# Three layers on one core: a chunked recurrence in blocks of 32, and projections in another order

## The chip, the cores and the metric

One core of a Trainium2 chip runs the whole program. Everything is fp32. The metric is the time of one execution in device microseconds; the kernel before took 1384.18 us (median of 3 runs, 1381.27 to 1385.24).

## The reference, cut to what matters

Three layers over 512 tokens of width 1024. The first two are "x + gate * rmsnorm(mixer(modulated rmsnorm(x)))"; layer 1 (L = 0 in the code) has latent attention (MLA, 8 heads, queries and keys through small latents cq and ckv) and windowed attention (SWA: sq, sk, sv, 8 query heads, 2 key heads); layer 2 (L = 1) has differential and forgetting attention. The third (L = 2, the "Mixer") has three kinds of sparse attention, stick-breaking attention, and HGRN2, the gated recurrence that most of the change is about:

```
b    = cumsum(log_f) within a chunk                        # per head and key channel
att[t, s] = sum_d q[t, d] key[s, d] exp(b[t, d] - b[s, d]) for s <= t
o    = att @ v + (q * exp(b)) @ state
state = exp(b_last) * state + (key * exp(b_last - b))^T @ v
o    = o * rsqrt(mean(o^2) + eps) * norm_w * silu(z)       # 6 heads of 64
x    = layer_norm(ALPHA * x + mixed @ w_out) * ln_g + ln_b
```

## The kernel before, in words

Tokens are tiled in T = 4 tiles of 128 (P). Each engine has one program in its own order; they meet at semaphores. On VectorE, ScalarE and Pool every operation waits for the one before it (`link`, `give`, `own`), so their times add up. Weights come through a ring of three slots of 2 MB (`ring`), filled by SyncE in the order of `chunks`; a slot is filled again when the last job of the chunk that it held is done (`chunk_end`). Products of weights and activations are jobs in one fixed order (`pr_plan`), the same on all engines: TensorE fills a PSUM bank, VectorE or ScalarE empties it. Before and between attentions jobs go round eight banks, beside an attention and in the last stage round two.

Layer 1 (TensorE's part, lines 1036 to 1089): cq and ckv (token-major, contraction of 8 blocks); their normalised tiles transposed (`cqT`, `ckvT`, copied by ScalarE); uq with the transposes `mqT`; ukv with `mkT`; then `roped` sq with `sqT` and skv with `skT` (VectorE rotates a tile, TensorE transposes it one tile later, ScalarE copies); gate0's first tile; then the attention. In `attention` (lines 922 and 1374 and 2028) each step handles one head's scores of one tile: TensorE makes the scores of a later step (`LOOK` = 2 ahead), filler work (projections of other parts, by `SPREAD`), the transposes of the weights, filler again, and the output of the step before. Score s has to wait until score s - 2 is masked. So the first step of an attention issues three scores, or four where they go in pairs.

The Mixer's attention has 88 steps, 72 to 87 of them stick-breaking; their fillers end with the part of the output projection whose inputs are ready (`mE`, `ye`: 5 of 8 contraction blocks). `HG_EARLY` names the steps behind which ScalarE makes the exponentials of chunks 0 and 1 of the recurrence. `close_behind` is where VectorE finishes a group of heads and frees its output bank.

The Mixer's stage (TensorE lines 1143 to 1215, VectorE 2301 to 2357, ScalarE 1590 to 1608, Pool 1651 to 1706) handles HGRN2 in 4 chunks of 128 tokens and 3 pairs of heads. exp(b[t] - b[s]) is not split over a whole chunk, but by levels: on level l the tokens go in blocks of 2^(l+1), the second half of a block looks at the first, and both are scaled relative to the border. Pool makes the differences, ScalarE their exponentials, Pool the products with key and query: 7 operands Y (levels 0 to 6), in two sets used in turn. TensorE multiplies for each level the operand by itself in two blocks of HB = 64 for both heads of the pair (`level_products`: 28 products of 64x64, and 2 for level 6, between the blocks); VectorE masks 7 of them (`levels`, 0 or 1) and adds them up into `att`, seven operations a pair, one of them the copy of level 6. TensorE then makes the chunk's outputs (`outputs`), and between these steps, `feed`, the rest of the output projection of the tile before (3 transposes and 6 products). VectorE then normalises the chunk's output (the "tail": copy, square, sum, rsqrt, scale, norm weights, gate), updates the state, and handles the layer norm of the tile two before (`output_tile`: ScalarE sums and squares, VectorE waits and scales, Pool applies ln_g and ln_b).

Of the kernel before, what the change touches and what calls it, by code (L numbers as in the profile page):

```python
# [31 lines left out]
P = 128  # L32
# [24 lines left out]
HB = 64  # L57
HP = 3
GW = NLEV * HB
# [16 lines left out]
def constants():  # L76
# [16 lines left out]
    for l in range(NLEV - 1):  # L93
        h = 1 << l
        lev.append((s // (2 * h) == t // (2 * h)) & (s % (2 * h) < h) & (t % (2 * h) >= h))
# [94 lines left out]
def pr_plan():  # L190
# [10 lines left out]
    def transposes(name):  # L201
        jobs.extend((name, i) for i in range(T))

# [131 lines left out]
HG_EARLY = (78, 84)  # L335
# [6 lines left out]
def two_block_kernel(nc, A, C, out):  # L342
# [15 lines left out]
    with ExitStack() as ctx:  # L358
# [67 lines left out]
        def carve(sizes):  # L426
            at, got = 0, {}
            for name, shape, rows in sizes:
# [35 lines left out]
        Y = [arena[:, o:o + NLEV * 384].rearrange("p (l m t) -> p l m t", l=NLEV, m=3)  # L464
             for o in (0, 2688)]
        slot = ring_slots(chunks)
        spare = ring[:, slot["w", "hi"], :]
        qb = [v.rearrange("p (m t) -> p m t", m=3) for v in (arena[:, 5376:5760], spare[:, 2048:2432])]
        kb = [v.rearrange("p (m t) -> p m t", m=3) for v in (arena[:, 5760:6144], spare[:, 2432:2816])]
# [4 lines left out]
        dec = [arena[:, 6528 + 4 * r:6531 + 4 * r] for r in range(2)]  # L474
# [11 lines left out]
        ktok = stage[:, 1536:3072].rearrange("p (b n) -> p b n", b=2)  # L486
        rtok = stage[:, 0:1024].rearrange("p (b n) -> p b n", b=2)
# [70 lines left out]
        gs_s = sem("gs_s")  # L558
        ho_done = sem("ho_done")
        hof = sem("hof")  # L560
        st_s = sem("st_s")
        ln_s = sem("ln_s")
        ln_q = sem("ln_q")
# [25 lines left out]
        def steps(L):  # L589
# [191 lines left out]
        def _(pe):  # L781
# [263 lines left out]
            for r in range(2):  # L1045
                b = begin(("relrow", r))
                pe.matmul(b[0:NSH, 0:320], tbl, onehot_r[:, 320 * r:320 * r + 320],
                          start=True, stop=True).then_inc(pr_done, 1)
            for i in range(T):
                if i == 0:  # L1050
                    drained(pe, ("ckv", T - 1))
                transposes(("cqT", i), [cqn[:, i, k * P:k * P + P] for k in range(3)])
            for i in range(T):
                transposes(("ckvT", i), [ckvn[:, i, k * P:k * P + P] for k in range(2)])
            drained(pe, ("ckvT", T - 1))
            for w, src, K, n, tr_name, tile in (("uq", a0["cqT"], 3, 384, "mqT", qtok),
                                                ("ukv", a0["ckvT"], 2, 512, "mkT", ktok)):
                W = weights(("w", w))
                for i in range(T + 1):
                    if i < T:  # L1060
                        for g in range(2):
                            token_major((w, i, g), W, i, n * g, n, src, K)
                    if i >= 1:
# [5 lines left out]
            def roped(name, n, nt, tile):  # L1069

                W = weights(("w", name[0]))
                for i in range(T + 1):
# [5 lines left out]
                    if i < T:  # L1078
                        token_major((name[0], i), W, i, 0, n)
                    if i >= 1:  # L1080
# [3 lines left out]
            roped(("sq", "sqT"), 512, 4, rtok)  # L1084
            roped(("skv", "skT"), 256, 1, rktok)
            whole_tile(("gate0", 0, 0))
            banks_back(pe, ("gate0", 0, 0))
# [55 lines left out]
            for c in range(T):  # L1143
                t = slice(c * P, c * P + P)
                pe.wait_ge(yr_s, c + 1)
                if c < T - 1:
                    transposes(("kbT", c), [kb[c % 2][:, m, :] for m in range(3)])

                def level_products(m):
                    n = c * HP + m  # L1150
                    if n >= 2:
                        pe.wait_ge(gm_s, n - 1)
                    for l in range(NLEV):
                        for j in range(2):
                            u = slice(HB * j, HB * j + HB)
                            for r in range(2):
                                q = slice(MN * r, MN * r + MN)
                                if l < NLEV - 1:
                                    a = b_ = Y[c % 2][q, l, m, u]
                                else:  # L1160
                                    w = slice(c * P + HB * j, c * P + HB * j + HB)
                                    a, b_ = a2["key"][q, m, w], a2["hq"][q, m, w]
                                pe.matmul(GB[n % 2][u, r, HB * l:HB * l + HB], a, b_, start=True, stop=True)
                    for r in range(2):
                        q = slice(MN * r, MN * r + MN)
                        mm = pe.matmul(GB[n % 2][0:HB, r, GW:GW + HB], Y[c % 2][q, NLEV - 1, m, 0:HB],
                                       Y[c % 2][q, NLEV - 1, m, HB:P], start=True, stop=True)
                    mm.then_inc(g_done, 1)

                def outputs(m):  # L1170
# [6 lines left out]
                    if c > 0:  # L1177

                        pe.matmul(OB[c % 2][:, m * P:m * P + P], qb[c % 2][:, m, :], state[:, m, :],
                                  start=True, stop=False)  # L1180
                    pe.wait_ge(gs_s, n + 1)
                    for r in range(2):
# [36 lines left out]
        def _(act):  # L1219
# [215 lines left out]
            def exponentials(c):  # L1435
# [3 lines left out]
                link(act.activation(Y[c % 2], Y[c % 2], ACT.Exp))  # L1439
                link(act.activation(kb[c % 2], kb[c % 2], ACT.Exp))  # L1440
                link(act.activation(qb[c % 2], a2["b"][:, :, t], ACT.Exp))
                if c >= 2:
                    act.wait_ge(pr_free[bank_of[prn["st", c - 2]]], nth[prn["st", c - 2]])
                give(act.activation(dec[c % 2], a2["b"][:, :, c * P + P - 1:c * P + P], ACT.Exp), ye_s, c + 1)

            def output_tile(i):
                drained(act, ("y", 2, i, 1))
                yb = ybuf2[:, i % 2, :]
                say(act.activation(tok[:, i, :], yb, ACT.Copy, accum_out=ss[:, 0:1]), sq_s, "sq_s")
                hear(mean_s, "mean_s")  # L1450
                say(act.activation(tok[:, i, :], yb, ACT.Square, bias=lam[:, 7:8], accum_out=ss[:, 0:1]), sq_s, "sq_s")
                rsqrt()
# [54 lines left out]
            for i in range(T):  # L1507
                for g in range(2):
# [12 lines left out]
            for i in range(T):  # L1521
                b = take(act, ("sqT", i))
                release(copy(a0["sqT"][:, :, i * P:i * P + P], heads(b[:, :])), ("sqT", i))
# [66 lines left out]
            for c in range(T + 1):  # L1590
# [9 lines left out]
                else:  # L1600
# [6 lines left out]
                if c < T:  # L1607
                    rsqrt(HGH)
# [15 lines left out]
        def _(pool):  # L1624
# [26 lines left out]
            def differences(c):  # L1651

                bc = a2["b"][:, :, c * P:c * P + P]
                if c >= 2:
                    pool.wait_ge(g_done, HP * (c - 1))
                    pool.wait_ge(ho_done, HP * (c - 1))
                for l in range(NLEV):
                    h = 1 << l
                    yl = Y[c % 2][:, l, :, :]
# [4 lines left out]
                tt(kb[c % 2], widen(last, P), bc, ALU.subtract).then_inc(y_s, 1)  # L1664
                pool.wait_ge(y_s, c + 1)

            def operands(c):
# [3 lines left out]
                for l in range(NLEV):  # L1671
                    h = 1 << l
                    yl = Y[c % 2][:, l, :, :]
                    own(tt(halves(yl, l, 0), halves(yl, l, 0), halves(a2["key"][:, :, t], l, 0), ALU.mult))
                    own(tt(halves(yl, l, h), halves(yl, l, h), halves(a2["hq"][:, :, t], l, h), ALU.mult))
                own(tt(kb[c % 2], kb[c % 2], a2["key"][:, :, t], ALU.mult))
                tt(qb[c % 2], qb[c % 2], a2["hq"][:, :, t], ALU.mult).then_inc(yr_s, 1)
# [22 lines left out]
            for c in range(T + 1):  # L1700
                if c + 2 < T:
# [728 lines left out]
```

## Time and profile before

| | |
|---|---|
| median of 3 runs | 1384.18 us |
| the profiled execution: its time, its span | 1384.93 us, 1383.4 us |
| busy: TensorE, VectorE, ScalarE, Pool | 1218.8, 557.7, 430.6, 106.0 us |
[...]

Durations are from that one execution. TensorE is busy in 88% of the span, but not evenly: the page's slices show nines through the layers and 6 to 8 in the last three of 40, where VectorE and Pool are busiest. An f32 matmul shows as two instructions. [...]

### The profile page before, as it was taken

What the parts mean: (1) busy time and instruction counts of PE and PEld (TensorE: products, weight loads), DVE (VectorE), ACT (ScalarE), POOL (GpSimd) and SP (SyncE); (2) the same over time, 40 slices, a digit from 0 to 9 for tenths busy, and PEclk for the clock granted to TensorE, in tenths of its full rate; (3) what the DMA queues carried; (4) which work ended last, traced back from release to release, by engine and by line L of the source; (5) the groups of instructions that cost most, each with busy time, mean ns of one, the idle gap of its engine ahead of it and who ended that gap; (6) DMA issues with size and microseconds to landing.
All of it is one profiled execution on the core that took longest, in us unless ns stands there. A gap on an engine that the chain in (4) does not pass through costs nothing.

```text
span 1383.4 us, 15153 instructions
## 1 busy us (share of the span) xinstructions
PE 1218.8 (88%) x5264; PEld 679.4 (49%) x5264; DVE 557.7 (40%) x1428; ACT 430.6 (31%) x1096; POOL 106.0 (8%) x138
## 2 busy tenths in 40 slices
PE   4879989999889898979999989989998999878654
PEld 1555454555554443334455555555453656545442
DVE  3234323334554311335442431122236532663885
ACT  0133014444451102232243322214343544660122
POOL 0000000000001000000000000000000000461752
PEclk8889989999998999999999989989999899998776
DMA  9321234562003412432111005241111011000001
GB/s 348 104 92 31 94 129 174 184 225 48 0 1 99 69 17 61 89 102 59 52 61 61 1 12 136 62 167 46 46 35 35 23 62 62 1 1 31 1 17 46
DMA packets 60402, 99.71 MB, mean 72 GB/s; under 512 B 12084, under 2 KB 22145, under 8 KB 60328
## 3 DMA queue, kind: packets, MB, share of 16 engines
q1 hardware_dynamic: 54514, 93.58, 22.1%
q10 hardware_dynamic: 5814, 5.18, 1.2%
q8 instruction: 43, 0.70, 0.2%
q14 instruction: 31, 0.25, 0.1%
HBM read 96.60 MB, written 4.08 MB: 73 GB/s over the span
## 4 chain that ended last, share of the span: by engine, by line
PE 74%; DVE 14%; ACT 5%; issue 2%; DMA 2%; ACTq 1%; DVEq 0%; SPq 0%
PE PR L905 32%; PE PT L798 6%; PE OB L935 6%; PE SC L957 6%; PE PR L798 5%; PE OB L798 4%; PE SC L798 4%; PE PT L972 3%; PE PR L860 3%; DVE stage L1735 2%; DMA ring<-in_w_ada 2%; DVE d L1735 1%; DVE tok L1735 1%; DVE ring L1735 1%; PE PR L813 1%
## 5 line engine op out<-in xcount | busy, mean ns | idle before, releaser
L905 PE MATMUL PR<-ring,hT 128*128 128x512 f32 (+1 forms) x784 | 376.4, 594 | 4.4 <-ACT hT L1244 3.5
L905 PEld LDWEIGHTS PR<-ring,hT 128*128 128x128 f32 x784 | 137.2, 198 | 104.8 <-issue 87.5
L1410 ACT ACTIVATE stage<-stage,nmax 128x256 f32<-128x256 f32 (+7 forms) x200 | 103.7, 519 | 268.1 <-DVE nmax L2087 237.8
L935 PEld LDWEIGHTS OB<-arena,pts 128*128 128x128 f32 (+3 forms) x880 | 129.1, 196 | 97.0 <-issue 76.2
L905 PE MATMUL PR<-hT,ring 128*128 128x512 f32 (+1 forms) x304 | 151.0, 622 | 0.0
L1643 POOL TENSOR_TENSOR arena<-arena 128x192 f32<-128x192 f32 (+1 forms) x118 | 78.6, 666 | 827.4 <-PE OB L935 758.0
L935 PE MATMUL OB<-arena,pts 128*128 128x64 f32 (+4 forms) x880 | 127.2, 273 | 9.2 <-ACT pts L1244 9.1
L957 PE MATMUL SC<-arena 64*128 64x256 f32 (+15 forms) x432 | 111.1, 447 | 10.2 <-DVE nmax L2087 10.2
L1244 ACT ACTIVATE pts<-PT 128x256 f32<-128x256 f32 (+7 forms) x200 | 80.7, 404 | 86.0 <-PE PT L972 63.5
L972 PEld LDWEIGHTS PT<-ident,stage 128*128 128x128 f32 (+3 forms) x440 | 58.6, 144 | 96.7 <-issue 69.5
L972 PE MATMUL PT<-ident,stage 128*128 128x128 f32 (+3 forms) x440 | 85.3, 285 | 13.1 <-DVE stage L1743 9.1
L2087 DVE CUSTOM_DVE_ANT_0 stage<-SC,causal 128x128 f32<-128x128 f32 (+3 forms) x96 | 47.1, 491 | 104.6 <-issue 55.0
L905 PEld LDWEIGHTS PR<-hT,ring 128*128 128x128 f32 (+1 forms) x304 | 51.4, 190 | 53.0 <-issue 51.7
L2087 DVE CUSTOM_DVE_ANT_0 stage<-SC,arena 128x128 f32<-128x128 f32 (+7 forms) x72 | 27.9, 388 | 96.1 <-PE SC L957 94.4
L957 PEld LDWEIGHTS SC<-arena 64*128 64x128 f32 (+2 forms) x432 | 45.9, 189 | 21.1 <-DVE nmax L2087 10.7
L798 PE MATMUL PR<-ring,hT 128*128 128x512 f32 (+5 forms) x160 | 50.6, 472 | 3.9 <-ACT hT L1287 2.0
L1739 DVE TENSOR_SCALAR t<-PR 128x512 f32<-128x512 f32 (+3 forms) x29 | 17.4, 600 | 85.3 <-PE PR L905 74.3
L798 PE MATMUL PT<-ring,hT 128*128 128x512 f32 (+4 forms) x144 | 50.0, 502 | 0.0
L860 PE MATMUL PR<-ring,tok 128*128 128x512 f32 x80 | 44.6, 690 | 6.0 <-ACT tok L1244 5.9
L798 PE MATMUL SC<-ring,hT 128*128 128x512 f32 (+3 forms) x144 | 48.0, 491 | 0.0
L1264 ACT ACTIVATE t<-t 128x512 f32<-128x512 f32 (+3 forms) x32 | 16.8, 525 | 73.7 <-DVE t L1739 73.6
L798 PEld LDWEIGHTS PR<-ring,hT 128*128 128x128 f32 x160 | 28.0, 199 | 23.3 <-issue 16.5
(346 smaller groups left out, 1332.1 us busy)
## 6 DMA issues: line engine op xcount, KB each, us to landing
ring<-in_w_ada SPq DMA_DIRECT2D x12, 2048.0 KB, 8.3
ring<-in_od_w_in SPq DMA_DIRECT2D x8, 2048.0 KB, 17.1
ring<-in_w_in SPq DMA_DIRECT2D x5, 1536.0 KB, 7.0
ring<-in_ev_w_in SPq DMA_DIRECT2D x3, 2048.0 KB, 7.8
ring<-in_w_in SPq DMA_DIRECT2D x3, 2048.0 KB, 9.9
ring<-in_ev_w_out SPq DMA_DIRECT2D x2, 2048.0 KB, 10.1
ring<-in_od_w_out SPq DMA_DIRECT2D x2, 2048.0 KB, 7.9
ring<-in_w_out SPq DMA_DIRECT2D x2, 2048.0 KB, 7.9
```

The lines of the kernel that those rows point to most:

```text
L798: mm = pe.matmul(dst, lhs(k), rhs(k), start=(k == 0), stop=(k == K - 1))
L860: mm = pe.matmul(b[:, :], tok[:, i, k * P:k * P + P], W[:, k, :], start=(k == 0), stop=(k == EARLY - 1))
L905: mm = pe.matmul(dst, l, r, start=(k == 0), stop=(k == KT - 1))
L935: mm = pe.matmul(ob[:, h * w:h * w + w], pts[0:rows_, v % 2, n * P:n * P + P], vb, start=(n == 0), stop=(n == len(blocks) - 1))
L957: pe.matmul(SC[s % 2][:, 0:n], q, k, start=True, stop=True).then_inc(s_done, 1)
L972: tr = pe.transpose(PT[v % 2][0:w, b * P:b * P + P], pb[:, s % NP, b * P:b * P + w], ident[:, :])
L1244: return act.activation(dst, src, ACT.Copy, scale=scale)
L1410: give(act.activation(pb[:, s % NP, 0:n], zm[:, s % 2, 0:n], ACT.Exp, bias=nmax[:, row, c:c + 1], scale=-1.0, accum_out=rsum[:, row, c:c + ...
L1643: return pool.tensor_tensor(dst, a, b, op)
L1735: return dve.tensor_tensor(dst, a, b, op)
L1739: return dve.tensor_scalar(dst, a, s1, None, op0)
L2087: give(dve.tensor_tensor_reduce(out=z, in0=SC[s % 2][:, 0:n], in1=mask, scale=-scale, scalar=start, op0=ALU.add, op1=ALU.min, accum_out=nm ...
```

## The change

Three edits. First, layer 1's projections: sq's weights come third, and its four tiles and their transposes go between the transposes of cq and ckv and the uq tiles, in a buffer of their own (`sqtok`, in tok); gate0's first tile goes ahead of the last skT. Second, in the attentions of layer 1 and the Mixer the first step looks one score ahead; the exponentials of chunks 0 and 1 come behind steps 75 and 82; a stick-breaking group is closed ahead of the step's scores; the norm's weights are multiplied onto the gate when that is made. Third, the Mixer's stage: blocks of 32, six levels masked (0 to 4 and the diagonal), and levels 5 and 6 copied into `att` by ScalarE; three sets of operands, so that Pool works through chunks 2 and 3 without waiting for the chunk just before; ScalarE squares the chunk's output from PSUM; the layer norm in steps between the head pairs, scaled by ScalarE; Pool's output tiles all behind chunk 3.

```diff
-HB = 64
-GW = NLEV * HB
+HB = 32
+GW = 6 * HB
-    transposes("cqT")
-    transposes("ckvT")
+    chunk(("w", "sq"), [("sq", 0)] + [("cqT", i) for i in range(T)] + [("sq", 1)] + [("ckvT", i) for i in range(T)]
+          + [("sqT", 0), ("sq", 2), ("sqT", 1), ("sq", 3), ("sqT", 2)])
...
+            if (w, i) == ("uq", 0):
+                u.append(("sqT", T - 1))
...
-    chunk(("w", "sq"), with_transposes("sq", "sqT"))
-    chunk(("w", "skv"), with_transposes("skv", "skT"))
+    chunk(("w", "skv"), with_transposes("skv", "skT")[:-1])
     jobs.append(("gate0", 0, 0))
+    jobs.append(("skT", T - 1))
...
-HG_EARLY = (78, 84)
+HG_EARLY = (75, 82)
...
-                upto = min(need + LOOK, s_all[-1])
+                upto = min(need + (1 if v == mine[0] and L != 1 else LOOK), s_all[-1])
...  (TensorE, layer 1)
-            banks_back(pe, ("gate0", 0, 0))
+            banks_back(pe, ("skT", T - 1))
...  (TensorE, level_products)
+                    for l in range(GW // HB):
+                        for b in range(P // HB):
+                            u = slice(HB * b, HB * b + HB)
+                            for r, q in enumerate(halves):
+                                ...
+                                pe.matmul(G[u, r, HB * l:HB * l + HB], k_, q_, start=True, stop=True)
+                    for j in range(2):
+                        for r, q in enumerate(halves):
+                            u = slice(64 * j, 64 * j + HB)
+                            pe.matmul(G[u, r, GW:GW + HB], y[5][q, m, u], y[5][q, m, 64 * j + HB:64 * j + 64],
+                                      start=True, stop=True)
+                    for r, q in enumerate(halves):
+                        mm = pe.matmul(G[0:64, r, GW + HB:GW + HB + 64], y[6][q, m, 0:64], y[6][q, m, 64:P],
+                                       start=True, stop=True)
...  (TensorE, outputs)
                     pe.wait_ge(gs_s, n + 1)
+                    pe.wait_ge(gc_s, n + 1)
...  (ScalarE)
+            def cross_blocks(c, m):
+                ...
+                act.wait_ge(gm_s, n + 1)
+                for j in range(2):
+                    u = slice(64 * j, 64 * j + HB)
+                    link(copy(w[u, :, 64 * j + HB:64 * j + 64], G[u, :, GW:GW + HB]))
+                give(copy(w[0:64, :, 64:P], G[0:64, :, GW + HB:GW + HB + 64]), gc_s, n + 1)
...
+            exponentials(2)
+            act.wait_ge(att_zero, 1)
+            for c in range(T):
                 ...      (kbT's and mT's copies as before)
+                cross_blocks(c, 0)
+                if c >= 2:
+                    norm_sum(c - 2)
+                cross_blocks(c, 1)
+                if c == 0:
                     for g in range(2):
                         mixed_ahead(T - 1, g)
-                if 1 <= c < T - 1:
-                    exponentials(c + 1)
                 if c >= 2:
-                    output_tile(c - 2)
+                    norm_square(c - 2)
+                if c == 2:
+                    exponentials(3)
+                cross_blocks(c, 2)
+                if c >= 2:
+                    norm_factor()
+                act.wait_ge(ho_done, HP * (c + 1))
+                give(act.activation(d2[:, 0:384], OB[c % 2][:, 0:384], ACT.Square), ho_sq, c + 1)
+                rsqrt(HGH)
+                if c >= 2:
+                    norm_scale(c - 2)
...  (Pool)
-                if c >= 2:
-                    pool.wait_ge(g_done, HP * (c - 1))
-                    pool.wait_ge(ho_done, HP * (c - 1))
+                if c >= 3:
+                    pool.wait_ge(g_done, HP * (c - 2))
+                    pool.wait_ge(ho_done, HP * (c - 2))
...  (VectorE)
+            def level_sums(n):
+                ...
+                give(tt(gm, G[:, :, 0:GW], ... levels ..., ALU.mult), gm_s, n + 1)
+                link(tt(gm[:, :, 0:3 * HB], gm[:, :, 0:3 * HB], gm[:, :, 3 * HB:6 * HB], ALU.add))
+                link(tt(gm[:, :, 0:HB], gm[:, :, 0:HB], gm[:, :, HB:2 * HB], ALU.add))
+                for b in range(P // HB):
+                    u = slice(HB * b, HB * b + HB)
+                    ins = tt(w[u, :, u], gm[u, :, 0:HB], gm[u, :, 2 * HB:3 * HB], ALU.add)
...  (chunk c)
+                level_sums(c * HP)
+                if c >= 2:
+                    norm_mean()
+                level_sums(c * HP + 1)
+                if c >= 2:
+                    norm_variance()
+                level_sums(c * HP + 2)
+                if c >= 2:
+                    norm_factor()
```

## Rows read from the trace of the kernel before

**Rows 1.** the page's chain of waits, shares of the span by engine

```profile
PE 74%; DVE 14%; ACT 5%; issue 2%; DMA 2%; ACTq 1%; DVEq 0%; SPq 0%
```

**Rows 2.** table by stretch: PE, PEld, DVE, ACT, POOL busy us, clock, DMA

```profile
1300.00:1383.00 83.00, 45.11 (x468) 28.41 (x466) 62.30 (x127) 18.39 (x40) 40.08 (x45) 0.73 0.07 26
```

**Rows 3.** TensorE's timeline, layer 1's projections: start, us, work [idle before]

```profile
89.33 0.66 PE L813 MATMUL SC<-ident,stage 128*128 128x128 f32 x3 [2.50 <-DVE arena L1735]
...
98.26 4.18 PE L798 MATMUL SC<-ring,arena 128*128 128x384 f32 x6 [4.87 <-ACT arena L1502]
102.23 4.56 PE L798 MATMUL PT<-ring,arena 128*128 128x384 f32 x12
...
139.33 7.03 PE L798 MATMUL SC<-ring,hT 128*128 128x512 f32 x16
...
171.05 5.30 PE L798 MATMUL SC<-ring,hT 128*128 128x256 f32 x16
176.19 3.62 PE L798 MATMUL PT<-ring,hT 128*128 128x256 f32 x16
...
199.82 0.80 PE L957 MATMUL SC<-arena 96*128 96x128 f32 x2 [3.58 <-DVE nmax L2087]
```

**Rows 4.** waits from 88 to 215 us: total us, times, longest

```profile
PE SC L813 <- DVE stage L1735: 3.8, 2, 2.3
```

**Rows 5.** the page's DMA issues: count, KB each, us to landing

```profile
ring<-in_ev_w_in SPq DMA_DIRECT2D x3, 2048.0 KB, 7.8
```

**Rows 6.** TensorE's and ScalarE's timelines, end of the Mixer's attention

```profile
1243.44 1.11 PE L813 MATMUL PR<-ident,tok 128*128 128x128 f32 x4 [4.82 <-DVE tok L1735]
...
1233.71 2.44 ACT L1439 ACTIVATE arena<-arena 128x2688 f32<-128x2688 f32 x1
```

**Rows 7.** VectorE's timeline: a row beside Pool, a head pair

```profile
1321.77 2.40 DVE L1735 TENSOR_TENSOR stage<-stage 128x384 f32<-128x384 f32 x3
...
1342.25 1.09 DVE L1735 TENSOR_TENSOR stage<-PT,grow 128x896 f32<-128x896 f32 x1
1343.38 0.28 DVE L2310 COPY ring<-PT 64x128 f32<-64x128 f32 x1
1343.69 1.21 DVE L1735 TENSOR_TENSOR stage<-stage 128x384 f32<-128x384 f32 x3
1344.94 0.61 DVE L1735 TENSOR_TENSOR ring<-stage 64x128 f32<-64x128 f32 x2
```

**Rows 8.** TensorE's timeline of the Mixer's stage

```profile
1258.43 1.04 PE L1163 MATMUL SC<-arena 64*64 64x64 f32 x56
...
1301.19 0.66 PE L1184 MATMUL OB<-arena,ring 128*128 128x64 f32 x4 [0.35 <-DVE ring L1735]
...
1346.64 1.77 PE L1163 MATMUL PT<-arena 64*64 64x64 f32 x56
...
1348.55 3.78 PE L996 MATMUL PR<-ring,hT 128*128 128x512 f32 x4
...
1352.95 1.94 PE L996 MATMUL PR<-ring,hT 128*128 128x512 f32 x4
```

**Rows 9.** VectorE's and TensorE's timelines, where the chunks and their tails begin

```profile
1280.09 0.56 DVE L2328 COPY d<-OB 128x384 f32<-128x384 f32 x1
...
1288.32 1.09 DVE L1735 TENSOR_TENSOR stage<-PT,grow 128x896 f32<-128x896 f32 x1
...
1312.90 1.09 DVE L1735 TENSOR_TENSOR stage<-SC,grow 128x896 f32<-128x896 f32 x1 [1.14 <-PE SC L1166]
...
1357.15 0.56 DVE L2328 COPY d<-OB 128x384 f32<-128x384 f32 x1
...
1364.87 0.87 PE L987 MATMUL PR<-ident,tok 128*128 128x128 f32 x3 [7.60 <-DVE tok L1735]
```

**Rows 10.** ScalarE's timeline, one operation of the last norm

```profile
1352.48 1.15 ACT L1451 ACTIVATE tok<-ring,lam 128x1024 f32<-128x1024 f32 x1 [9.44 <-DVE lam L1739]
```

**Rows 11.** Pool's timeline, the multiplications of chunk 3

```profile
1320.21 10.19 POOL L1643 TENSOR_TENSOR arena<-arena 128x192 f32<-128x192 f32 x14 [4.03 <-ACT arena L1444]
```

More of the change, by code:

```diff
@@ L92, in constants @@
     s, t = np.arange(P)[:, None] % HB, np.arange(HB)[None, :]
-    for l in range(NLEV - 1):
+    for l in range(GW // HB - 1):
         h = 1 << l
@@ L473, in two_block_kernel @@
         kbT = arena[:, 6144:6528]
-        dec = [arena[:, 6528 + 4 * r:6531 + 4 * r] for r in range(2)]
+        dec = [arena[:, 6528 + 4 * r:6531 + 4 * r] for r in range(3)]
         state = arena[:, 6656:7040].rearrange("p (m e) -> p m e", m=3)
@@ L558, in two_block_kernel @@
         gs_s = sem("gs_s")
+        gc_s = sem("gc_s")
         ho_done = sem("ho_done")
@@ L1048, in _, with swa_transposes @@
                           start=True, stop=True).then_inc(pr_done, 1)
+            W = weights(("w", "sq"))
+            def swa_transposes(i):
+                drained(pe, ("sq", i))
+                transposes(("sqT", i), [sqtok[:, i % 2, k * P:k * P + P] for k in range(4)])
+            token_major(("sq", 0), W, 0, 0, 512)
             for i in range(T):
@@ L1052, in _ @@
                 transposes(("cqT", i), [cqn[:, i, k * P:k * P + P] for k in range(3)])
+            token_major(("sq", 1), W, 1, 0, 512)
             for i in range(T):
                 transposes(("ckvT", i), [ckvn[:, i, k * P:k * P + P] for k in range(2)])
+            for i in range(T - 1):
+                swa_transposes(i)
+                if i + 2 < T:
+                    token_major(("sq", i + 2), W, i + 2, 0, 512)
             drained(pe, ("ckvT", T - 1))
@@ L1079, in roped @@
                         token_major((name[0], i), W, i, 0, n)
+                    if i == T and name[0] == "skv":
+                        whole_tile(("gate0", 0, 0))
                     if i >= 1:
@@ L1507, in _ @@
             for i in range(T):
+                b = take(act, ("sqT", i))
+                release(copy(a0["sqT"][:, :, i * P:i * P + P], heads(b[:, :])), ("sqT", i))
+            for i in range(T):
                 for g in range(2):
@@ L1699, in _ @@
             operands(1)
-            for c in range(T + 1):
-                if c + 2 < T:
-                    differences(c + 2)
-                if c + 2 < T:
-                    operands(c + 2)
-                if 1 <= c < T:
-                    output_tile(c - 1)
+            for c in range(2, T):
+                differences(c)
+                operands(c)
+            for i in range(T - 1):
+                output_tile(i)
         @block.vector
@@ L2094, in attention @@
                     finish_gates()
-                    if r_:
+                    if r_ and not stick_end:
                         close_behind(v - 1)
@@ L2177, in _ @@
                 if i >= 2:
+                    used(dve, ("sqT", i - 2))
+                b = take(dve, ("sq", i))[:, :].rearrange("p (n w) -> p n w", n=NH)
+                u, w = rope(None, b, NH, MN, cosh_[:, i, :], sinh_[:, i, :])
+                dst = sqtok[:, i % 2, :].rearrange("p (j v d) -> p v j d", j=4, v=2)
+                four = lambda z: z.rearrange("p (v j) d -> p v j d", v=2)
+                for kv in range(2):
+                    ins = tt(dst[:, kv, :, :], four(u)[:, kv, :, :], four(w)[:, kv, :, :], ALU.add)
+                    if kv == 0:
+                        link(ins)
+                release(ins, ("sq", i))
+            for i in range(T):
+                if i >= 2:
                     used(dve, ("mqT", i - 2, 1))
```

197 lines of the change are left out of this document (95 added, 102 removed).

## The prediction, made before the changed kernel ran

> **What bounds the kernel now.** I read the chain of waits first, by engine: TensorE holds 74% of it and VectorE 14% [rows 1]. The reader should take from it that there are two kinds of stretch. [...] Then TensorE's timeline for the projections of layer 1 (L = 0 in the code), and VectorE's and TensorE's for the Mixer's stage.
>
> **Part 1: projections of layer 1.** TensorE waits 2.50 us for the normalised ckv before the first transposes, and 4.9 us before uq's first product. That product runs slow: its 6 instructions take 4.18 us, where the next 12 take 4.56: 1.9 lost [rows 3]. The last transposes of sq and of skv wait 3.8 us in two waits [rows 4], and after the first of them skv's first product takes 5.30 against 3.62: 1.7 lost [rows 3]. Sum: 2.5 + 4.9 + 1.9 + 3.8 + 1.7 = 14.8 us. In the new order an sq product of 6.9 us (the 128x512 pattern of rows 3) stands in front of the cq transposes, another in front of the ckv transposes, so ScalarE's copies of cqT and ckvT (8 us) run beside sq(1) and sq(2); the last sqT stands behind uq(0), and gate0's first tile in front of the last skT. Each gap has at least 3.9 us of products in it, against chains on VectorE of at most 2.6 us (an sq tile's rotation, the longest). Added: a wait for the last skT's copy on ScalarE before the first scores, 0.6 us, behind which all of TensorE stands. Net 14.2.
>
> Transfers: sq's 2 MB now load third, into the slot that the modulation's fourth chunk leaves, some 45 us before use. SyncE's queue is past skv's wait at about 120. The gate's first 2 MB are issued behind the last ukv product, about 17 us before use, behind two rows of 0.5 MB; 7.8 us to landing is what such a chunk takes [rows 5]. Hidden; if not, a few us.
>
> First step with two scores: TensorE now waits 3.58 us at the third score, because VectorE first finishes the gate [rows 3]. Without it the filler's first part runs in that time and the first transpose comes when its weights are ready, some 4.7 us behind the gate's tile instead of 6.8; the score (0.4) still has to be done. Gain 1.7; in the Mixer's attention the same with smaller tiles, 0.4.
>
> **Part 2: the end of the Mixer's attention.** TensorE stands 4.82 us for VectorE's closing of a stick-breaking group. In front of it ScalarE made chunk 1's exponentials: 2.44 us and three small ones, 3.9 in all [rows 6]. Now these come two steps earlier, where VectorE and ScalarE both idle behind slow products, and the group is closed ahead of the next tail. That takes 4.8 away. Chunk 0's exponentials come three steps earlier, in steps of 2.7 us that have no slack on ScalarE: a new stall of up to 3.9, I take 3.0. The four products with the norm's weights (0.56 us each on VectorE) move here beside TensorE's work: 0, at most 2.3. Net gain 1.8 (bounds: loss 3, gain 5).
>
> **Part 3: the Mixer's stage.** Per head pair VectorE took 1.09 + 0.28 + 1.21 + 0.61 with gaps = 3.33 us [rows 7]. From the 896 column and the 128 column rows an operation costs about 0.15 + 0.00105 us a column. The new seven (384, 192, 64, and four of 64 columns) then cost 0.55 + 0.35 + 5 x 0.22 + gaps 0.2 = 2.2. So 12 x 1.1 = 13 us leave VectorE. But they are not on the path all the time: in chunk 1 TensorE's last outputs waited only 0.35 us for VectorE [rows 8], so its own row of work (outputs, level products, six projection products at half clock and then full clock) was as long: from 1288.32 + 3.35 to 1301.85, 10.2 us. That is what is late next.
>
> Price of the new level products. Before: 56 instructions of 64x64 take 1.04 us at the high level, 1.77 at the low one: 18.6 and 31.6 ns each [rows 8]. As a + b and a + 2b that is 5.6 fixed and 13.0 that goes with the clock. Now there are 108 instead of 60, nearly all of 32 columns. If nothing of the 13.0 shrinks: 2.0 us fast, 3.4 slow. If it shrinks with both sizes (to a quarter): 1.0 and 1.3. I take half, 12 and 19 ns: 1.3 and 2.0, where it was 1.1 and 1.9: nothing. No row has such a tile; the ends go into the range.
> [...]
>
> Tail of a chunk (outputs read until the gated result): 384 column operations are 0.56 us each [rows 9]. A copy, a square and the weights' product leave VectorE, ScalarE's square (0.5) comes: net 1.1. Pool's work no longer falls on all of it; with Pool beside it three sums took 2.40 instead of 1.21 [rows 7]. The state's 6 small operations become 4 wider ones, 0.3.
>
> Chunk by chunk, on starts of operations of VectorE (the last: TensorE) [rows 7 to 9]:
> - Chunk 0 (until 1280.09) is TensorE's: ten projection products. The first now wait for the copies of mixed behind the second head pair on ScalarE instead of for VectorE: 1.5 earlier (bounds 0 and 5, the latter if the clock no longer falls).
> - 1280.09 to 1288.32, 8.2: now 4.9. Gain 3.3.
> - Chunk 1 until its outputs are there, 1301.85 [rows 8], 13.5: now 2.2 + 0.7 beside Pool + 10.2 = 13.1. Gain 0.4.
> - to 1312.90, 11.05: now tail 4.4, residual half 0.7, then kbT's transposes and a level product, 2.9. Gain 3.0.
> - Chunk 2 and its tail, to 1342.25, 29.35. ScalarE's order is mT's copy, cross blocks, the norm's sum (1.15 [rows 10]), cross blocks, its square, the exponentials of chunk 3 (3.9), cross blocks. VectorE waits for the mean until about T+5.1 and for the square until T+8.1; the exponentials end at T+12.0, the third cross blocks at 12.9, the outputs at 13.5, the factor's part on VectorE at 15.0. Pool multiplies only from T+12.0 and needs 12.4 (14 in 10.19 us [rows 11] and two more). TensorE waits for that at T+24.4, and the first products of chunk 3 take 1.9: T+26.4. Gain 2.95. So a new wait, for Pool, takes most of what VectorE saves.
> - Chunk 3 to 1357.15, 14.9: now 3.8 + 9.8 + 0.6. Gain 0.7.
> - Tail 3 to 1364.87, 7.7: now 4.7. Gain 3.0.
> - The rest, 18.5 us, goes by TensorE's 12 products and the last norm, which are unchanged: 0.
> Sum of part 3: 14.85.
>
> All: 14.2 + 2.1 + 1.8 + 14.9 = 33.0 us. The profiled execution took 1384.93, 0.75 over the median of 1384.18: 1384.93 - 33.0 = 1351.9, or 1351 on the median.
>
> **Rivals.**
> Small products cost as much as large ones. TensorE's path holds about nine groups of level products in the stage, the two of chunk 0 at the high level (+0.7), seven at the low one (+1.4), of which some 2 are hidden: +9, 1360. For: the fixed cost per instruction is real and the count doubles. Against: the part that goes with the clock, 13 of 18.6 ns, is array time, and half as many columns stream and load.
> The clock stays up. VectorE's shorter pauses could spare TensorE the half clock: 3.78 us for four instructions of a projection against 1.94 [rows 8], in chunks 0 to 3 and the end, and the low prices of the level products: 10 us less, 1341. Against: it still idles over 4 us in each tail.
> The first part is not had in full, because the gate's or the modulation's chunk lands late or banks come back late: 7 to 9 us less, 1359.
> The other side: the 32 column tiles don't run beside each other. It lies in level products alone. At the 0.43 us that one full instruction takes (6.9 us for 16 [rows 3]), a quarter of it for 128 columns in place of 512, 0.11 us, a head pair takes 11.7 us and 12 of them 125 more: about 1476. It decides from 33 / 12 = 2.8 us more for a head pair, 36 ns an instruction. Against: the 64x64 products already come every 18.6 ns, on four tiles.
>
> **How the numbers follow.** Forecast 0.56; small products dear 0.19; clock 0.12; part 1 short 0.09; the other side 0.04. All but the last are faster by over 0.3% (4.2 us, which is about what a measurement of this kernel can tell); 0.01 is for sums of mishaps that end within it: 0.95, 0.01, 0.04. The range goes from the clock's case to the dear products with some of part 1 missing: 1340 to 1365.
>
> **What would show it.** Part 1: no TensorE gap over 1.5 us between 86 us and the first scores, these at about 181 instead of 195.6. Part 2: the 4.8 us wait gone, one of some 3 near step 75. Part 3: VectorE near 2.2 us a head pair, VectorE starts of chunks 1 and 2 some 24 us apart become some 21; TensorE or Pool, not VectorE, ends the waits in chunks 2 and 3; an idle time of TensorE for Pool before chunk 3. I am wrong if a head pair's level products exceed 2.5 us at the low level, or if chunk 3 starts less than 24 us or more than 29 after chunk 2.

## The result, and the profile after

The changed kernel takes 1368.01 us (median of 4, 1365.65 to 1372.01) against 1384.71 us before: ratio 0.9877, 95% interval [0.9848, 0.9905]. The same kernel timed again beside later experiments gave 1363.70 (6 runs, 1360.40 to 1368.97) against 1385.11: 0.9855 [0.9832, 0.9878]. So it gains 17 to 20 us where 33 were forecast. The forecast of 1351 was wrong, and so was its range of 1340 to 1365.

The profiled execution has a span of 1363.9 us, 19.5 less than before's 1383.4. Its chain of waits by engine, against [rows 1]:

```profile
PE 77%; DVE 11%; ACT 5%; issue 2%; DMA 2%; ACTq 1%; POOL 1%; DVEq 0%; SPq 0%; POOLq 0%
```

The last 83 us in the table by stretch, against [rows 2]:

```profile
1280.90:1363.90 83.00, 50.39 (x880) 31.60 (x880) 48.76 (x130) 29.55 (x72) 27.73 (x26) 0.75 0.07 27
```

VectorE fell from 62.3 to 48.8 us and ScalarE rose from 18.4 to 29.6: the work was moved as the diff says. Before, this was a stretch in which VectorE was busy longer than TensorE; now TensorE is, 50.4 against 48.8. In the last three of the page's 40 slices TensorE's busy tenths went from 6, 5 and 4 to 8, 6 and 5, its granted clock from 7, 7 and 6 to 8, 7 and 7. TensorE's timeline of layer 1's projections, against [rows 3]:

```profile
86.74 7.13 PE L804 MATMUL SC<-ring,hT 128*128 128x512 f32 x16
...
137.73 0.61 PE L819 MATMUL PR<-ident,stage 128*96 128x128 f32 x4 [1.21 <-ACT arena L1270]
...
172.69 7.10 PE L911 MATMUL PR<-ring,hT 128*128 128x512 f32 x16 [1.63 <-DVE stage L1800]
...
180.33 0.71 PE L963 MATMUL SC<-arena 96*128 96x128 f32 x4 [0.43 <-ACT arena L1270]
...
184.41 0.33 PE L978 MATMUL PT<-ident,stage 128*128 128x128 f32 x1 [2.37 <-ACT stage L1436]
```

The gaps of 2.50 and 4.87 us are gone; the first scores come at 180.33 instead of 195.63, 15.3 earlier. The end of the Mixer's attention, on TensorE, against [rows 6]:

```profile
1182.81 0.69 PE L978 MATMUL PT<-ident,stage 128*128 128x128 f32 x2 [3.20 <-ACT stage L1408]
1183.30 2.77 PE L911 MATMUL PR<-ring,hT 128*128 128x384 f32 x4
...
1193.22 2.04 PE L866 MATMUL PR<-ring,tok 128*128 128x512 f32 x2 [0.83 <-ACT tok L1270]
...
1236.41 0.46 PE L819 MATMUL PR<-ident,tok 128*128 128x128 f32 x1 [3.61 <-DVE x L1808]
...
1252.31 0.99 PE L1184 MATMUL SC<-arena 64*32 64x32 f32 x94
```

The first level products start at 1252.31 against 1258.43, only 6.1 earlier. At step 75 of the Mixer's attention, just ahead of the first of these rows, the lead over before had been 12.6. So in the stretch of part 2, which was to gain 1.8, 6.5 were lost.

The Mixer's stage, against [rows 7 to 9]: VectorE's starts of chunks 1, 2 and 3, one head pair, and TensorE in front of and behind chunk 3.

```profile
1279.36 0.56 DVE L1800 TENSOR_TENSOR stage<-PT,grow 128x384 f32<-128x384 f32 x1
...
1280.83 2.64 DVE L1800 TENSOR_TENSOR ring<-stage 32x64 f32<-32x64 f32 x4
...
1299.01 0.56 DVE L1800 TENSOR_TENSOR stage<-SC,grow 128x384 f32<-128x384 f32 x1 [0.76 <-PE SC L1191]
...
1304.28 0.56 DVE L1800 TENSOR_TENSOR stage<-PT,grow 128x384 f32<-128x384 f32 x1
1304.87 0.62 DVE L1800 TENSOR_TENSOR stage<-stage 128x192 f32<-128x192 f32 x2
1305.52 0.97 DVE L1800 TENSOR_TENSOR ring<-stage 32x64 f32<-32x64 f32 x4
...
1325.00 0.56 DVE L1800 TENSOR_TENSOR stage<-PT,grow 128x384 f32<-128x384 f32 x1 [4.11 <-PE PT L1191]
1325.59 2.65 DVE L1800 TENSOR_TENSOR stage<-stage 128x192 f32<-128x192 f32 x2
```

The last of these rows in a narrower view, and what Pool does at that time:

```profile
1325.98 2.26 DVE L1800 TENSOR_TENSOR stage<-stage 128x64 f32<-128x64 f32 x1
...
1325.59 2.57 POOL L1710 TENSOR_TENSOR x<-ring,arena 128x1024 f32<-128x1024 f32 x1
```

```profile
1323.14 1.16 PE L1184 MATMUL PT<-arena 64*32 64x32 f32 x92 [8.05 <-POOL arena L1710]
...
1324.82 1.16 PE L1184 MATMUL SC<-arena 64*32 64x32 f32 x92
...
1345.01 0.52 PE L993 MATMUL PR<-ident,tok 128*128 128x128 f32 x3 [4.53 <-DVE tok L1800]
```

| stretch | before | after | gain | forecast |
|---|---|---|---|---|
| first level products to chunk 1 | 29.9 | 27.1 | 2.8 | 4.8 |
| chunk 1 to 2 | 24.6 | 19.7 | 4.9 | 3.4 |
| chunk 2 to 3 | 29.4 | 26.0 | 3.4 | 2.95 |
| chunk 3 to TensorE behind its tail | 22.6 | 20.0 | 2.6 | 3.7 |
| rest | 18.5 | 18.9 | -0.4 | 0 |

Sum 13.3 against 14.85. A head pair takes VectorE 2.2 us as forecast (0.56, 0.62 and 0.97 from 1304.28; beside Pool the last is 2.64 and the middle one 2.65). The 108 instructions of a head pair's level products (54 in the kernel, each two in the trace) take 1324.82 - 1323.14 = 1.68 us at the low level (granted clock 0.50 from 1323.1 to 1326), from the first of one pair to the first of the next: 15.6 ns each. And the new wait for Pool is there, 8.05 us.

### The profile page after: what moved, and what is told of

Its sections match the earlier page's. It is cut to its first block, busy times and chain, and to the rows that moved or that the text cites. A ratio compares the mean times of both kernels' runs of the same rounds, so it can differ in the third digit from the quotient of the medians.

```text
span 1363.9 us, 16366 instructions
## 1 busy us (share of the span) xinstructions
PE 1218.7 (89%) x5840; PEld 677.9 (50%) x5840; DVE 538.3 (39%) x1412; ACT 445.1 (33%) x1140; POOL 105.5 (8%) x138
## 4 chain that ended last, share of the span: by engine, by line
PE 77%; DVE 11%; ACT 5%; issue 2%; DMA 2%; ACTq 1%; POOL 1%; DVEq 0%; SPq 0%; POOLq 0%
PE PR L911 33%; PE OB L941 6%; PE SC L963 6%; PE PT L804 5%; PE PR L804 5%; PE OB L804 5%; PE SC L804 4%; PE PT L978 3%; PE PR L866 3%; DMA ring<-in_w_ada 2%; PE PR L1002 1%; DVE tok L1800 1%; DVE stage L1800 1%; POOL arena L1710 1%; DVE arena L2025 1%
## 5 line engine op out<-in xcount | busy, mean ns | idle before, releaser
L911 PEld LDWEIGHTS PR<-ring,hT 128*128 128x128 f32 x784 | 138.0, 199 | 106.6 <-issue 89.4
L1710 POOL TENSOR_TENSOR arena<-arena 128x192 f32<-128x192 f32 (+1 forms) x90 | 60.5, 673 | 823.8 <-PE OB L941 761.4
L804 PE MATMUL PR<-ring,hT 128*128 128x512 f32 (+5 forms) x176 | 55.9, 473 | 3.9 <-ACT hT L1313 2.0
L963 PEld LDWEIGHTS SC<-arena 64*128 64x128 f32 (+2 forms) x432 | 46.3, 192 | 15.6 <-issue 4.4
L804 PEld LDWEIGHTS PR<-ring,hT 128*128 128x128 f32 x176 | 30.4, 195 | 25.5 <-issue 18.8
L804 PE MATMUL PT<-ring,hT 128*128 128x512 f32 (+4 forms) x128 | 42.9, 491 | 0.0
```

The source lines that it names most:

```text
L804: mm = pe.matmul(dst, lhs(k), rhs(k), start=(k == 0), stop=(k == K - 1))
L911: mm = pe.matmul(dst, l, r, start=(k == 0), stop=(k == KT - 1))
L963: pe.matmul(SC[s % 2][:, 0:n], q, k, start=True, stop=True).then_inc(s_done, 1)
L1710: return pool.tensor_tensor(dst, a, b, op)
```

## The experiments

Each run gives two readings: the median against the kernel before on the same chip (one kernel's runs spread over 4 to 14 us), and the trace. Kernels that share their code up to some instruction are aligned on its k-th occurrence; "lead" is the difference of the two times there. Where a stretch of one trace is compared with the same stretch of another, what the two had gained or lost ahead of it drops out.

**The three parts alone.** The kernel before with one part of the diff each.

> The kernel before with part 1 alone: the projections of layer 1 in the new order, everything else as before. The changed kernel's trace has its first scores 15.3 us earlier than before (180.3 against 195.6), but its lead is smaller 200 to 700 us later, with the same waits, because the granted clock stays low longer after them. Theory A (clock by chance of place): first scores 15 us earlier again, and of these 11 to 15 are left at the end: 1370 to 1374 against 1384.7. Rival B (a cost that the new order causes further on, in a transfer or a bank that comes later): the same five stretches lose the same 5 us, at the same instructions as in the changed kernel: 1374.5. My forecast before the result, 14.2, gives 1370.5.

> The kernel before with part 2 alone: chunk 0's exponentials at step 75 and chunk 1's at 82 in place of 78 and 84, and the end of a stick-breaking group put ahead of the next scores. Theory A (part 2 costs): a wait of some 3 us of TensorE near step 75 with half the clock behind it, and the 4.82 us wait gone: first level products 4 to 7 us later than before, 1389 to 1391. Forecast of the prediction: 1.8 faster, 1383. Rival B: the loss of 6.5 us in the changed kernel came from the rest of it (VectorE's tails beside Pool, the four products with the norm's weights), then this kernel is within 2 us of the kernel before.

> The kernel before with part 3 alone: the Mixer's stage rebuilt, with its three sets of operands and the four products with the norm's weights in the attention, chunk 0's and 1's exponentials still at steps 78 and 84. Theory A: the stage is 13.4 us shorter as in the changed kernel's trace, and the attention's end is as before: 1371 to 1373. Rival B (the norm's weights and the wider Pool work cost part of the 6.5 us at the end of the attention): first level products 2 to 4 us later than before, 1374 to 1376. The prediction's 14.85 gives 1370.

| kernel | median | before | ratio [95%] | effect |
|---|---|---|---|---|
| part 1 | 1370.07 | 1384.44 | 0.9899 [0.9877, 0.9921] | -14.0 |
| part 2 | 1389.77 | 1384.44 | 1.0044 [1.0029, 1.0059] | +6.1 |
| part 3 | 1372.77 | 1384.44 | 0.9921 [0.9898, 0.9944] | -10.9 |

The effects (one minus the ratio, of 1384.44) add up to 18.8 us, as much as the whole change. Part 1's first scores came at 180.09, 15.5 earlier. Part 3's span was 15.6 less, of which a lead of 2.8 was there at step 75, before its stage began; the other 12.8 lie inside the interval of its median. Part 2 is the surprise. Its timeline of TensorE:

```profile
1190.17 0.69 PE L972 MATMUL PT<-ident,stage 128*128 128x128 f32 x2 [3.20 <-ACT stage L1382]
...
1200.58 2.04 PE L860 MATMUL PR<-ring,tok 128*128 128x512 f32 x2 [0.83 <-ACT tok L1244]
...
1222.67 1.56 PE L860 MATMUL PR<-ring,tok 128*128 128x512 f32 x2 [2.44 <-ACT tok L1244]
...
1243.67 0.48 PE L813 MATMUL PR<-ident,tok 128*128 128x128 f32 x1 [3.61 <-DVE x L1743]
```

The same waits as in the changed kernel (3.20, 0.83, 3.61), without any of part 3. From step 75 to the level products its lead over before goes from +5.3 to -1.1, 6.4 lost, against 6.5 in the changed kernel. So the loss is part 2's own, and theory A holds. (The +5.3 before step 75 stands on identical code; see the clock below.)

**Which step is dear.**

```
-HG_EARLY = (75, 82)
+HG_EARLY = (78, 82)
```

> The changed kernel with chunk 0's exponentials at step 78, where the kernel before had them, and chunk 1's still at 82. Theory A (the step 75 is dear: a wait of 3.2 us and then 14 us at half the clock): the stall near step 75 is gone, the 4.82 us wait stays away, first level products 5 to 8 us earlier than in the changed kernel: 1360 to 1363 against its 1368. Rival B (the stall only moves to step 78, as TensorE has no slack there either): within 1.5 us of the changed kernel, 1367 to 1369.

1371.79 us, 0.9902 [0.9879, 0.9925]: no better. The trace says why: the stall at 75 went (lead over the changed kernel from +2.4 to +10.8), and behind step 82 all of it was lost (+0.7). ScalarE and Pool there:

```profile
1213.91 2.44 ACT L1466 ACTIVATE arena<-arena 128x2688 f32<-128x2688 f32 x1 [8.01 <-POOL ring L1710]
...
1188.32 24.60 POOL L1710 TENSOR_TENSOR arena<-arena 128x192 f32<-128x192 f32 x30 [14.67 <-ACT arena L1471]
1212.99 0.83 POOL L1710 TENSOR_TENSOR ring<-arena 128x384 f32<-128x384 f32 x1
```

Pool works 25.5 us on `operands(0)` and `differences(1)`, the products of chunk 0 and the differences of chunk 1, between the two exponentials. With four steps between them ScalarE stands 8.01 us at its head of queue, and TensorE 6.84 behind it. So the two steps are tied: a second exponential at 82 needs the first well ahead of 78, and my theory A for this run left that out.

```
-HG_EARLY = (75, 82)
+HG_EARLY = (78, 84)
```

> The changed kernel with both exponentials back at steps 78 and 84; the end of a stick-breaking group still ahead of the next scores. The run with step 78 and 82 showed ScalarE 8.01 us waiting for Pool, which needs 25.5 us between the two. Theory A (where ScalarE's and Pool's work falls is the whole cost of part 2, the early close is good): from step 75 to the first level products 6 to 9 us less than the changed kernel, 1360 to 1362 against 1368. Rival B (the early close itself costs: TensorE's wait of 3.61 us for VectorE's closed tile was made by it): 2 to 4 us less only, 1364 to 1366.

The second of this pair keeps (78, 84) and also puts the closing of a group back:

```
-                    if stick_end:
-                        close_behind(v - 1)
...
-                    if r_ and not stick_end:
+                    if r_:
```

> The changed kernel without part 2: steps 78 and 84, and the stick-breaking group closed where it was. Theory A: from step 75 to the first level products as in the run of part 3 alone (a wait of 5.2 us for VectorE near 1238, but no wait of 3.2 near step 75): 5 to 6.5 us less than the changed kernel, 1362 to 1363. Rival B (the early close itself costs): this one is faster than the kernel with 78 and 84 and the early close by 2 to 4 us, 1360 to 1362.

With the early close 1357.40 us, 0.9822 [0.9798, 0.9846]; without it 1361.61, 0.9839 [0.9814, 0.9863]. The stall of 3.20 us is gone in both traces. TensorE's waits near the second exponentials, with the early close and then without it:

```profile
1225.40 0.66 PE L978 MATMUL PT<-ident,stage 128*128 128x128 f32 x4 [1.49 <-ACT stage L1408]
1228.90 0.48 PE L819 MATMUL PR<-ident,tok 128*128 128x128 f32 x1 [2.85 <-DVE x L1808]
```

```profile
1233.84 1.12 PE L819 MATMUL PR<-ident,tok 128*128 128x128 f32 x4 [5.16 <-DVE tok L1800]
```

The early close turns one wait of 5.16 us into two of 1.49 and 2.85. The stretches of the traces:

| kernel | step 75 to the level products | step 75 to the end of the span |
|---|---|---|
| before | 80.6 | 205.6 |
| part 2 alone | 87.0 | 212.4 |
| changed | 87.1 | 198.7 |
| 78 and 84, early close | 80.5 | 191.7 |
| 78 and 84, closed where it was | 81.1 | 191.8 |

So the steps cost 6.6 us up to the level products. Behind the stall 8.4 had been lost; 1.8 come back, because the later waits are shorter in the changed kernel. The early close gains 0.6 there and 0.1 by the end: nothing that can be told apart. Part 2's loss is the steps'. By the ratios the first of the pair is 0.0033 to 0.0055 below the changed kernel, 4.6 to 7.6 us, which agrees with the traces' 6.6 to 6.9. Between the two of the pair the intervals overlap.

**The wait for Pool.** ScalarE makes chunk 3's exponentials in its idle time at the end of chunk 1.

```
+                if c == 1:
+                    exponentials(3)
...
-                if c == 2:
-                    exponentials(3)
```

> The changed kernel with one move: ScalarE makes chunk 3's exponentials behind the last cross blocks of chunk 1, where it idles 4.17 us, and not in chunk 2. Pool can then multiply some 15 us earlier. Theory A (Pool ends the wait before chunk 3, as the prediction said; what is late next is TensorE's own work, VectorE idles 4.11 us there): chunk 3 starts 22 to 23 us behind chunk 2 where it took 26.0, so 3 to 4 us less, 1364 to 1365. Rival B (contention): Pool's 16 operations now fall beside VectorE's tail of chunk 1, whose small operations take up to 2.7 times as long, and give back 2 to 3 us: within 1.5 us of 1368.

1358.64 us, 0.9822 [0.9791, 0.9852]. TensorE in front of chunk 3:

```profile
1308.45 0.99 PE L1184 MATMUL PT<-arena 64*32 64x32 f32 x94
...
1309.73 0.99 PE L1184 MATMUL SC<-arena 64*32 64x32 f32 x94
```

No wait for Pool, and the granted clock is 1.00 from 1308.4 to 1311: 108 instructions in 1.28 us, 11.9 ns each. The lead over the changed kernel is 6.4 us all through chunks 0 and 1 (from the clock of the layers before) and 10.8 at TensorE's last projection products: 4.4 are the move's. By the end of the span it is 5.5 (193.2 us from step 75 against 198.7). The other 1.0 lies behind TensorE's last product, where the traces here took 9.2 to 10.9 us, so it may not be the move's. Beside Pool the tail of chunk 1 gives back 0.8 up to the first level products of chunk 2; the lead is down to 4.3 some 8 us later and back at 6.2 before chunk 3. So the loss that rival B named is there for a while, but it does not last.

**Two scores in the first step.**

```
-                upto = min(need + (1 if v == mine[0] and L != 1 else LOOK), s_all[-1])
+                upto = min(need + LOOK, s_all[-1])
```

> The changed kernel with three scores again in the first step of each attention. Prediction: 1.7 us later behind the first step of layer 1 and 0.4 in the Mixer's. The changed kernel's trace gave 2.3 in the first and nothing in the second, where TensorE waits 2.90 us all the same. Theory A: 2.3 later in layer 1, within 0.3 in the Mixer's apart from the clock: 1370. Rival B (two scores save nothing, the 2.3 was the clock): both within 0.5.

1367.88 us, 0.9884 [0.9854, 0.9914], the same within its interval. Its first step of layer 1, from the first scores to the first value product, is 0.55 us longer in the trace (10.76 against 10.21). Against before it is 2.3 shorter in the changed kernel, but 1.8 of that are there with three scores too: the wait for the third score is 2.78 us behind the new order of part 1, where it was 3.58, and the rest was clock. In the Mixer's attention nothing can be told apart. Neither theory had the size.

**Both moves together, and the changed kernel again.**

> The changed kernel unchanged, timed again beside the two others. Theory A (the 5 us that its first profiled run lost between the first value product and step 75 are granted clock that differs from run to run): median 1365 to 1369, the distance between the same two instructions other than 974.7 us by up to 5, with TensorE's idle time in the stretch of layer 1 still 28 us. Rival B (they are a fixed cost of the new order): 974 to 976 again.

> The changed kernel with both moves that helped: exponentials of chunks 0 and 1 at steps 78 and 84, and those of chunk 3 behind the last cross blocks of chunk 1. Theory A (they lie in different stretches and add up: 8.0 of the one, 4.4 of the other by the traces): 1354 to 1357. Rival B (chunk 3's come beside a chunk 1 that is later relative to Pool's differences, so ScalarE waits for Pool and the gain of the second is lost): 1359 to 1361.

> As the kernel with both moves, and three scores again in the first step of the Mixer's attention, two in layer 1's alone. Theory A (two scores cost 1.5 us there: the wait for VectorE is 2.9 us either way, and less work is left beside it): 1.5 us less than the kernel with both moves, 1352 to 1355. Rival B (that 1.5 was the clock of single runs): the same as that kernel within 1.

With both moves 1351.15 us (1345.88 to 1356.89) against 1385.11: 0.9756 [0.9733, 0.9779]. Beside it the changed kernel ran at 1363.70, so they bring 12.5 us. From step 75 to the end of the span its trace takes 186.3 us, 12.3 less than the changed kernel's; the two moves alone took 6.9 and 5.5 off, 12.4 together. That is the best version here. Three scores in the Mixer's first step gave 1357.09 (1345.85 to 1359.89), 0.9788 [0.9760, 0.9816]: no gain. Between two value products around that step it takes 117.6 us, with two scores 117.8: the 1.5 that I had read was the clock. A warning comes with these sums. The changed kernel took 198.66 and 198.65 us from step 75 to the end in its two traces, but this last kernel took 189.6, 3.3 more than the one with two scores, though they differ only in a step 250 us ahead. So one trace of the last stretch is good to some 3 us, and that 12.3 meets 12.4 is in part luck.

**The clock.** The stretch between the first value product of layer 1 and one of the next layer's, in the tables of four kernels (before, part 1 alone, the changed kernel, the changed kernel again):

```profile
208.20:567.00 358.80, 330.35 (x1280) 175.71 (x1279) 130.32 (x339) 117.87 (x313) 6.95 (x2) 0.96 0.29 84
```

```profile
190.80:554.40 363.60, 335.69 (x1279) 178.43 (x1278) 130.23 (x339) 117.87 (x313) 6.95 (x2) 0.95 0.29 83
```

```profile
190.60:552.30 361.70, 333.74 (x1279) 177.72 (x1278) 130.31 (x339) 117.94 (x313) 6.95 (x2) 0.96 0.29 82
```

```profile
191.50:551.70 360.20, 331.84 (x1279) 176.50 (x1278) 130.28 (x339) 117.86 (x313) 6.95 (x2) 0.96 0.29 82
```

TensorE's idle time is 28.5, 27.9, 28.0 and 28.4 us, and VectorE's and ScalarE's work is the same to 0.1. What grows is TensorE's busy time: the same instructions at a lower granted clock. One place shows it best. The same product behind the same wait, before and in part 2 alone, where the code up to there is identical:

```profile
795.69 1.57 PE L905 MATMUL PR<-ring,hT 128*128 128x512 f32 x2 [1.04 <-ACT hT L1244]
797.05 1.06 PE L972 MATMUL PT<-ident,stage 128*128 128x128 f32 x4
797.91 2.72 PE L905 MATMUL PR<-ring,hT 128*128 128x512 f32 x4
```

```profile
793.02 1.10 PE L905 MATMUL PR<-ring,hT 128*128 128x512 f32 x2 [1.04 <-ACT hT L1244]
793.95 0.60 PE L972 MATMUL PT<-ident,stage 128*128 128x128 f32 x4
794.39 1.88 PE L905 MATMUL PR<-ring,hT 128*128 128x512 f32 x4
```

In the one the granted clock is 0.50 for 2.5 us and more from 797, behind a wait of 1.04 us (0.68 in the 4 us from 797), in the other it is 1.00 in the same 4 us: 1.7 us between them. From the first value product to step 75 the seven traces of kernels with the changed kernel's code there took 968.8 (twice), 971.3, 971.4, 972.2, 974.7 and 975.0: the first profiled run of the changed kernel, 974.7, was nearly the slowest, and before's own 969.7 lies inside (the two kernels with its code there: 967.2 and 967.4). The second trace of the changed kernel is one of the two at 968.8. Between the two traces of the changed kernel TensorE's busy time there went from 911.9 to 904.6 us and its idle time from 62.8 to 64.2. So theory A holds: the 5 us lost there are no fixed cost. One thing stays open. In the stretch of layer 1 alone three traces of the old order took 358.5 to 358.8, ten of the new 360.1 to 364.9. Of these ten the eight with two scores in the first step took 360.1 to 360.2 (three) or 361.6 to 361.9 (five), some 1.6 apart, as much as one fall of the clock cost above; the two with three scores took 363.6 and 364.9, so the first step may have a part in it. The idle time is the same, so it is clock too, but why the new order should always meet it later I did not settle. What makes the clock fall in one run and not in another the traces do not show.

## Why the prediction was wrong

Right: what bounds each stretch (with the last 83 us as the one where VectorE was busy longer, 62.3 us of them against TensorE's 45.1 [rows 2]), the direction, part 1, VectorE's price of a head pair, the wait for Pool with its place (8.05 us in front of chunk 3). Wrong: the sum, by 13 to 16 us. The parts alone miss by 7.9 (part 2), 4.0 (part 3), 1.5 (two scores) and 0.2 (part 1).

- **Part 1**, 14.2 forecast: 14.0 [10.9, 17.0] alone, 15.5 at its first scores. Held, though the agreement to 0.2 is in part luck: the first scores gained more than forecast, and the clock took some of it in layer 1's stretch. Up to the first scores TensorE has no new wait for a transfer or a bank, so the rival of a first part not had in full falls. "No gap over 1.5 us" was missed slightly (1.63, and 2.37 behind the scores).
- **First step with two scores**, 1.7 and 0.4: 0.55 and nothing. The wait of 3.58 us that it was to save had become shorter by part 1 already, and 2.37 us of wait, now for ScalarE, were left.
- **Part 2**, 1.8 gained: 6.1 lost. This is the step that failed, more than half of the error, and outside my own bound of a loss of 3. "A new stall of up to 3.9, I take 3.0" had the stall (3.20) and left out what comes behind it: from there to 1199 the granted clock is 0.50, and the lead falls from 12.6 to 6.4 by 1193.22. I had charged such a stretch elsewhere (1.9 behind a gap of 4.87) but not here. "That takes 4.8 away" failed too: 3.61 of the 4.82 us of wait are left. Read from the trace, VectorE's last chain for the group is as long as before or longer: its operations (0.96, 1.90 and 1.30 us, the middle one a scan) took 0.79, 1.58 and 0.90 before. They run beside Pool, which ScalarE's earlier exponentials started earlier (`operands(1)` at 1219 to 1235). That Pool is the reason for the wait is argued and not shown: with the exponentials back at 78 and 84 the chain was as fast as before, and the waits were 1.49 and 2.85. And I asked only what the exponentials delay, not what they are tied to: Pool's 25.5 us between them.
- **Part 3**, 14.85: 13.3 in the trace, 10.9 [7.8, 14.1] alone. By stretch it was 2.0 short up to chunk 1, 1.5 over in the next, 0.4 over in the third, 1.1 short up to TensorE behind tail 3. There a product that I priced at 0.56 took 2.67 (1342.19 to 1344.86) beside Pool's product for the output tile (1342.11 to 1344.45). The mechanisms held, the sizes were somewhat too large; that Pool's product is what cost the last 1.1 is read from the two rows and was not tested.
- **Level products**, 12 and 19 ns: 11.9 and 15.6. No row had such a tile, and that "half" came so near at the high level is luck. The rival of dear small products falls: at the low level a head pair's 108 instructions take 1.68 us where it wanted 3.4. An instruction of 32 columns costs less than one of 64 at both levels (11.9 ns against 18.6, 15.6 against 31.6). How much of it is fixed and how much is the array's no run separates: the forecast's 5.6 and 13.0 ns are an estimate from the two rows of 64x64. As the tiles also went from four to eight, these rows say nothing of one tile alone. The rival of tiles that don't run side by side falls with it.
- **The clock stays up**: this rival falls too, 0.75 over the last 83 us against 0.73.

Beside the terms stands the measurement: one profiled run moves by some 6 us with the clock alone (968.8 to 975.0), and a forecast made on one trace has that uncertainty before any term is wrong. My range had nothing for it.

## What to carry to other kernels

A stall that an edit makes in front of a busy TensorE can cost more than its length: here 3.20 us of wait, 1.5 of which came back at the next one, and a granted clock of 0.50 from there to 1199 cost 6.2, and moving the step back gained 6.6. Not each wait lowered the clock: behind the 1.63 us at 172.69 it was 1.00 up to 180. When work of one engine is moved earlier, follow its chain through the other engines to the next thing that waits for it: two exponentials with 25.5 us of Pool between them could not be moved one by one (8.01 us of waiting in the run that tried). When a kernel has places where ScalarE idles (4.17 us behind chunk 1), a late operation that another engine waits for belongs there; that one move gained 4.4 us. When VectorE has small operations with all operands in SBUF on the critical path, look at how long Pool's instructions beside them are: here 0.62 us became 2.65 beside one of 2.57.

## What the runs showed of the hardware

- In the kernel before four instructions of a 128x512 product took 3.78 us at a granted clock of 0.50 (from 1348.5 to 1352.3) and 1.94 at 1.00 (from 1352.9 to 1354.9) [rows 8]; so TensorE's busy time has to be read together with its clock.
- Tiles of 64x32 in float32, with inputs from halves of 64 partitions and outputs on quarters of 32 (L1184), came every 11.9 ns at a granted clock of 1.00 and every 15.6 at 0.50, counted per instruction. From 0.50 to 1.00 the time shrank to 0.76. Against tiles of 64x64 (18.6 and 31.6 ns) it shrank to 0.64 at 1.00 and to half at 0.50.
- Small VectorE operations with all inputs in SBUF suffered most beside Pool: four sums of 32x64 took 2.64 us instead of 0.97, and two, of 128x192 and 128x64, took 2.65 instead of 0.62. Operations on 384 columns that read PSUM kept their 0.56, as that at 1279.36, with Pool busy from 1274.59 to 1283.39. The price went by Pool's instruction and not by VectorE's: the sum of 128x64, 0.22 us alone, began at 1325.98 behind the start of a Pool instruction of 2.57 us and ended at 1328.24, 0.08 us behind Pool's end. The four sums of 32x64 ended 0.07 to 0.08 us behind the end of a Pool instruction each.
- The same code took from 968.8 to 975.0 us in seven traces, and behind the same wait of 1.04 us the clock fell in one and stayed up in another.
